# Scoring the two heads of a sliding-window pair on two 64-row tiles of TensorE, with a projection slot between two halves of the scores

## The reference

```python
s = jnp.einsum('bnqhgd,bnshd->bnhgqs', qb, kk) * scale      # 128 queries against 256 keys, per block and head
s = s - alibi_slopes(B_QHEADS).reshape(...) * dist
s = jnp.where(valid[None, :, None, None], s, NEG)
p = sink_softmax(s, sinks)                                  # softmax over the keys and one sink logit
o = jnp.einsum('bnhgqs,bnshd->bnqhgd', p, vv)
```

## Time and profile before

| what | value |
|---|---|
| three runs | 1378.04, 1379.92, 1379.98 us (median 1379.92) |
| span of the profiled execution, first to last instruction | 1374.8 us |
| the median run less this span | 5.1 us |
| TensorE busy, mean granted clock | 1324.7 us (96%), 0.991 |
| VectorE, ScalarE, GpSimd busy | 602.9, 519.1, 259.8 us |
| the sliding stage, 8 pairs | 775.6 us to about 1082 us |

### The profile page before, as it was taken

How to read it: one execution, slowest core, us unless ns; L and a number is a source line. 1 busy time by engine, 2 the same in 40 slices (tenths; PEclk the granted TensorE clock), 3 DMA queues, 4 the chain that set the end, 5 groups by cost and what they waited for, 6 DMA issues and landing times.

```text
span 1374.8 us, 23499 instructions
## 1 busy us (share of the span) xinstructions
PE 1324.7 (96%) x9150; PEld 1252.4 (91%) x9150; DVE 602.9 (44%) x1239; ACT 519.1 (38%) x1022; POOL 259.8 (19%) x119
## 2 busy tenths in 40 slices
PE   5799999999999999999999999999999999999998
PEld 4799999999999999899999988988988899999885
DVE  6636566574746465500000444555554400445222
ACT  6343635445353535511111434455444422313111
POOL 0222222222322222222222111011011022242000
PEclk9899999999999999999999999999999999999999
DMA  5212121202021221111112310111110312141231
GB/s 190 64 31 64 32 64 32 76 17 76 17 76 47 62 63 34 49 44 46 46 46 51 81 31 15 31 31 24 22 31 1 87 33 61 46 113 41 92 129 47
DMA packets 136750, 73.61 MB, mean 54 GB/s; under 512 B 37185, under 2 KB 133138, under 8 KB 136690
## 3 DMA queue, kind: packets, MB, share of 16 engines
q1 hardware_dynamic: 136706, 72.99, 19.0%
HBM read 63.77 MB, written 10.22 MB: 54 GB/s over the span
## 4 chain that ended last, share of the span: by engine, by line
PE 67%; issue 22%; POOL 5%; ACT 3%; DVE 3%; DMA 0%; SPq 0%; DVEq 0%; POOLq 0%; ACTq 0%
PE pj L970 46%; POOL w_l L556 4%; PE pj L986 3%; PE pj L1311 2%; PE ps_d L1201 1%; PE ps_e L1201 1%; PE ps_a L1311 1%; PE ps_e L1311 1%; PE ps_b L1189 1%; PE ps_c L1311 1%; PE ps_d L1311 1%; PE ps_b L1311 1%; PE ps_a L1189 1%; PE ps_a L1166 1%; PE ps_c L1189 1%
## 5 line engine op out<-in xcount | busy, mean ns | idle before, releaser
L970 PE MATMUL pj<-xn_h,w_h 128*128 128x352 f32 x1704 | 562.6, 330 | 10.9 <-DVE q L1384 5.3
L970 PE MATMUL pj<-xn_h,w_l 128*128 128x352 f32 x1704 | 552.0, 324 | 0.0
L970 PE MATMUL pj<-xn_l,w_h 128*128 128x352 f32 x1704 | 551.7, 324 | 0.0
L556 POOL TENSOR_TENSOR w_l<-w_raw,w_h 128x1024 fp32r<-128x1024 f32 x82 | 202.2, 2466 | 731.0 <-ACT w_h L628 731.0
L970 PEld LDWEIGHTS pj<-xn_h,w_h 128*128 128x128 f32 x1704 | 324.3, 190 | 15.7 <-DVE q L1384 5.6
L970 PEld LDWEIGHTS pj<-xn_l,w_h 128*128 128x128 f32 x1704 | 324.8, 191 | 0.3
L970 PEld LDWEIGHTS pj<-xn_h,w_l 128*128 128x128 f32 x1704 | 323.7, 190 | 0.0
L628 ACT ACTIVATE w_h<-w_raw 128x1024 fp32r<-128x1024 f32 x82 | 86.4, 1054 | 114.7 <-PE pj L970 99.8
L1546 DVE TENSOR_TENSOR mg<-sg,pj 128x352 f32 (+1 forms) x24 | 12.4, 522 | 151.7 <-PE pj L970 150.2
L837 ACT ACTIVATE scores<-scores,stat 128x256 f32<-128x256 f32 (+1 forms) x128 | 61.4, 481 | 0.0
L970 PE MATMUL pj<-hl_h,w_l 128*128 128x352 f32 x168 | 54.3, 323 | 0.0
(11 more groups left out here) (363 smaller groups left out, 2095.6 us busy)
## 6 DMA issues: line engine op xcount, KB each, us to landing
w_raw<-in_w_in_dram SPq DMA_DIRECT2D x132, 256.0 KB, 3.4
x_t<-in_x_prompt_dram SPq DMA_DIRECT2D x8, 512.0 KB, 8.5
s<-in_state_hgrn_dram SPq DMA_DIRECT2D x8, 512.0 KB, 4.2
out_dram<-s SPq DMA_DIRECT2D x8, 512.0 KB, 3.2
w_raw<-in_w_pa_dram SPq DMA_DIRECT2D x16, 256.0 KB, 2.9
w_raw<-in_w_pb_dram SPq DMA_DIRECT2D x16, 256.0 KB, 4.4
wo_raw<-in_w_out_dram SPq DMA_DIRECT2D x8, 512.0 KB, 4.0
x_o<-in_x_prompt_dram SPq DMA_DIRECT2D x8, 512.0 KB, 4.1
```

The lines of the kernel that those rows point to most:

```text
L556: g.tensor_tensor(w_l[p][:], w_raw[p][:], w_h[p][:].bitcast(F32), ALU.subtract).then_inc(w_lo_ready, 1)
L970: mm = nc.tensor.matmul(pj[g][:, 0:W], w[:, kt, :], x[:, kt, span(g)], start=(kt == 0 and m == 0), stop=(kt == KT - 1 and m == 2))
```

## The change

- The keys are kept once: `kT` is `[128, 1056]`. A score matmul takes 64 rows of `qT` and of `kT`: rows 0 to 63 for head 0, 64 to 127 for head 1, and the two heads of a block write different banks. The zero fill of `kT` in the prologue goes, three of six copies of the keys on ScalarE, and two of four transposes for the cache output.
- The scores go by quarters of two blocks (`scores_of(k)`): quarters 0 and 1, a slot, quarters 2 and 3, a slot.
- `sk` goes (VectorE and ScalarE read `sinks` directly); `qs` and `zs` go to ScalarE, ahead of the exponentials.
- Outs and turns go in rounds of three blocks, with one slot of the next gate between rounds.
- The loops over pairs are written out on TensorE, VectorE and ScalarE.

```diff
-        score_bank = lambda n, h: ((ps_a, ps_b, ps_c, ps_d)[n % 4], h * 2 * P)
+        head_rows = lambda h: slice(h * HD, (h + 1) * HD)
+        score_bank = lambda n, h: ((ps_a, ps_b, ps_c, ps_d)[n // 2 % 2 * 2 + h], n % 2 * 2 * P)
...
-                for n in range(NC):
-                    if n >= 4:
-                        t.wait_ge(dve_done, dve.at(now, f"t{2 * (n - 4) + 1}"))
-                    for h in range(2):
-                        bank, o = score_bank(n, h)
+                def scores_of(k):
+
+                    if k >= 2:
+                        t.wait_ge(dve_done, dve.at(now, f"t{QU * (k - 2) + QU - 1}"))
+                    for n in (2 * k, 2 * k + 1):
                         lo = P if n == 0 else 0
-                        mm = nc.tensor.matmul(bank[:, o + lo:o + 2 * P], qT[:, n * P:(n + 1) * P],
-                                              kT[:, h, (n - 1) * P + lo:(n + 1) * P], start=True, stop=True)
-                    mm.then_inc(pe_done, pe.tick(now, f"s{n}"))
+                        for h in range(2):
+                            bank, o = score_bank(n, h)
+                            mm = nc.tensor.matmul(bank[:, o + lo:o + 2 * P], qT[head_rows(h), n * P:(n + 1) * P],
+                                                  kT[head_rows(h), (n - 1) * P + lo:(n + 1) * P], start=True, stop=True)
+                    mm.then_inc(pe_done, pe.tick(now, f"s{k}"))
...
-                for g in range(2):
-                    next_slot(g)
+                scores_of(0)
+                scores_of(1)
+                next_slot(0)
+                scores_of(2)
+                scores_of(3)
+                next_slot(1)
...
-                for n in range(3):
+                for n in blocks_of(0):
                     turn(n)
                 next_slot(2)
-                for n in range(NC):
-                    out(n)
-                    if n + 3 < NC:
-                        turn(n + 3)
-                if not last:
-                    for g in range(SLOTS):
-                        t.wait_ge(act_done, act.at(now, f"q{g}"))
-                        slot(B(3), g)
+                for r in rounds:
+                    for n in blocks_of(r):
+                        out(n)
+                    for n in blocks_of(r + 1):
+                        turn(n)
+                    if not last:
+                        t.wait_ge(act_done, act.at(now, f"q{r}"))
+                        slot(B(3), r)
...
-                v.tensor_copy(sink_m[:].rearrange("p (h m) -> p h m", h=2), sinks[:].rearrange("p (h m) -> p h m", h=2)[:, :, bass.ds(m, 1)])\
-                 .then_inc(dve_done, dve.tick(now, "sk"))
-                v.wait_ge(dve_done, dve.at(now, "b1"))
-                v.tensor_copy(q_s[:, :, bass.ds(m, 1), :], qT[:, SEQ:T].rearrange("p (b o t) -> p b o t", b=NB, o=1)).then_inc(dve_done, dve.tick(now, "qs"))
```

More of the change, by code:

```diff
@@ L108, in hybrid_step @@
     exps = [x for k in quarters for x in [f"es0_{k}", f"es1_{k}"] + units("p", k)]
-    softmax = (["b0", "b1", "sk", "qs"] + [x for k in quarters for x in units("t", k) + [f"nm0_{k}", f"nm1_{k}"]] + ["zs"]
+    softmax = (["b0", "b1"] + [x for k in quarters for x in units("t", k) + [f"nm0_{k}", f"nm1_{k}"]]
                + [x for k in quarters for x in [f"dn{k}", f"rd{k}"] + units("n", k)])
-    turn_order = ["t0", "t1", "t2"] + [x for n in range(NC) for x in [f"o{n}"] + ([f"t{n + 3}"] if n + 3 < NC else [])]
+    blocks_of = lambda r: range(3 * r, min(3 * r + 3, NC))
+    rounds = range(3)
+    turn_order = [f"t{n}" for n in blocks_of(0)] + [x for r in rounds for x in [f"o{n}" for n in blocks_of(r)]
+                                                    + [f"t{n}" for n in blocks_of(r + 1)]]
     norms = ["rl0", "rl1", "rls", "rx"]
@@ L121, in hybrid_step @@
          + ["sigq1", "sigq2"] + each_slot("sigz"), HEADS - 1, len(norms)),
-        ("last", norms + exponentials + turned + [f"k{g}{h}" for g in range(SLOTS) for h in "ab"] + squares_of_head
+        ("last", norms + exponentials + turned + each_slot("k") + squares_of_head
          + each_tile("h", 0, 3) + each_slot("sg") + each_tile("h", 3, 5) + ["fl0", "fl1", "fls", "fx"] + each_tile("h", 5), 1, 0),
@@ L163, in hybrid_step @@
         ("kv", ["vt0", "vt1", "vts", "kt"], 1, 0),
-        ("swa", [f"s{n}" for n in range(NC)] + turn_order, HEADS - 1, 0),
-        ("swa_l", [f"s{n}" for n in range(NC)] + turn_order, 1, 0),
+        ("swa", [f"s{k}" for k in quarters] + turn_order, HEADS - 1, 0),
+        ("swa_l", [f"s{k}" for k in quarters] + turn_order, 1, 0),
         ("swa_s", ["ct0", "ct1", "s0", "s1", "s2", "s3", "pt", "pn", "o"], 1, 0),
@@ L743, in head @@
                         a.wait_ge(slot_done, B(1)[0] * 3 + (g + 1))
-                        for h in range(2):
-                            rows_h = slice(h * HD, (h + 1) * HD)
-                            a.activation(kT[rows_h, h, span(g)], pj[g][rows_h, 0:W], ACT.Copy).then_inc(act_done, act.tick(now, f"k{g}{'ab'[h]}"))
+                        a.activation(kT[:, span(g)], pj[g][:, 0:W], ACT.Copy).then_inc(act_done, act.tick(now, f"k{g}"))
                     split_hi(B(3))
@@ L816, in _ @@
             a.wait_ge(pe_done, pe.at(here, "kt"))
-            two_heads = lambda a: a.rearrange("p (h x) -> p h x", h=2)[:, :, 0:HD]
-            a.activation(k_out[:, 0, :].rearrange("p (h d) -> p h d", h=2), two_heads(ps_d[:, 0:6 * HD]), ACT.Copy).then_inc(act_done, act.tick(here, "kt"))
-            a.activation(k_out[0:NS, 1, :].rearrange("p (h d) -> p h d", h=2), two_heads(ps_e[0:NS, 0:6 * HD]), ACT.Copy).then_inc(act_done, act.tick(here, "ks"))
+            a.activation(k_out[:, 0, :], ps_d[:, 0:P], ACT.Copy).then_inc(act_done, act.tick(here, "kt"))
+            a.activation(k_out[0:NS, 1, :], ps_e[0:NS, 0:P], ACT.Copy).then_inc(act_done, act.tick(here, "ks"))
             split_hi(qz(2))
@@ L844, in pair @@
                 if not last:
-                    a.wait_ge(pe_done, pe.at(now, "s7"))
-                    a.wait_ge(dve_done, dve.at(now, "qs"))
+                    a.wait_ge(pe_done, pe.at(now, "s3"))
+                    a.wait_ge(act_done, act.at(now, "qs"))
                 for g in range(2):
@@ L849, in pair @@
                 for n in range(0, NC, 2):
[L850 removed]
+                    if n == 4:
                         queries(2)
@@ L865, in pair @@
                     split_hi(B(5))
-            with nc.scalar.Fori(0, HEADS - 1) as m:
+            for m in range(HEADS):
                 pair(m)
-            pair(HEADS - 1)
             here = ("swa_s", 0)
@@ L1037, in gate_slot @@
                         return
-                    step = f"k{g}b" if last and k_block == 2 else f"{name}{g}"
+                    step = f"k{g}" if last and k_block == 2 else f"{name}{g}"
                     t.wait_ge(by[0], by[1].at(now, step))
@@ L1143, in _ @@
             nc.tensor.transpose(ps_c[0:NS, 0:P], zb[:, SEQ:T], ident[:, :]).then_inc(pe_done, pe.tick(here, "vts"))
[L1144 to L1147, removed]
+            nc.tensor.transpose(ps_d[:, 0:P], kT[:, SEQ - P:SEQ], ident[:, :])
+            nc.tensor.transpose(ps_e[0:NS, 0:P], kT[:, SEQ:T], ident[:, :]).then_inc(pe_done, pe.tick(here, "kt"))
             for g in range(SLOTS):
@@ L1203, in out @@
                     mm.then_inc(pe_done, pe.tick(now, f"o{n}"))
-                for n in range(3):
+                for n in blocks_of(0):
                     turn(n)
                 next_slot(2)
-                for n in range(NC):
-                    out(n)
-                    if n + 3 < NC:
-                        turn(n + 3)
-                if not last:
-                    for g in range(SLOTS):
-                        t.wait_ge(act_done, act.at(now, f"q{g}"))
-                        slot(B(3), g)
+                for r in rounds:
[6 more added lines that the diff above has]
+                        slot(B(3), r)
             t.wait_ge(act_done, act.at(("kv", 0), "ks"))
             t.wait_ge(dve_done, dve.at(("kv", 0), "vt1"))
-            with nc.tensor.Fori(0, HEADS - 1) as m:
+            for m in range(HEADS):
                 pair(m)
-            pair(HEADS - 1)
             here, gb = ("swa_s", 0), Blocks(GB, 2, 0)
@@ L1243, in _ @@
                     nc.tensor.matmul(bank[32 * j:32 * j + 32, o:o + P], q_m, ckT[rows_h, m, :], start=True, stop=True)
-                    mm = nc.tensor.matmul(bank[32 * j:32 * j + 32, o + P:o + P + NS], q_m, kT[rows_h, h, SEQ:T], start=True, stop=True)
+                    mm = nc.tensor.matmul(bank[32 * j:32 * j + 32, o + P:o + P + NS], q_m, kT[rows_h, SEQ:T], start=True, stop=True)
                 mm.then_inc(pe_done, pe.tick(here, f"s{u}"))
@@ L1562, in _, with negate @@
                 gated(here, "z", g, zb)
-            def negate(now, k, new, old, sink, scores_next=len(quarters)):
+            def negate(now, k, new, old, sink):
```

(10 more changed lines are left out.)

34 lines of the change are left out of this document (16 added, 18 removed).

## The result

The changed kernel takes **1344.55 us** (median of 4 runs, 1343.57 to 1347.82), the kernel before beside it 1379.95 (1378.04 to 1381.16): a ratio of 0.9747, 95% interval 0.9732 to 0.9762. That is 35.4 us faster; 33.5 were forecast, and the time lies in the range.

A forecast was written before the change was run, and what follows sets the result against it. TensorE, busy 96% of the span, bounds the kernel. A pair saves 1.65 + 2.9 + 0.2 - 0.5 = 4.25 us; eight save 34.0, less 0.5 in the last, 33.5: 1346.4 us, range 1339 to 1361.

The forecast's parts named there:

- the new wait: TensorE ahead of turn 2 waits for VectorE's division of block 2: about 0.5 us a pair, between 0 and 1.2.
- the scores: Two 64-row tiles side by side take a pair's score matmuls from 6.5 to 3.6 us: 2.9 us saved.
- the loops: Pair loops written out: neither fetching new code nor the jump back shows, so nothing was counted.
- the stop: In each pair block 4's score matmuls wait for VectorE to empty a bank: 1.65 us saved, refill included.
- The ratio of the outs: Outs on two column halves take 0.57 of the whole-array time a record; used to estimate the row tiles' overlap.
- Boundaries: Changes between array shapes on TensorE, 0.12 us each, go from 12 to 10 a pair: 0.2 us saved.
- The last pair: No slot stands between rounds there, so two outs wait for copies of their turns: about 0.5 us lost once.
- Rival 1: The two row tiles of the score matmuls do not overlap: 1365.6 us; no or half an overlap has chance 0.17.
- Rival 3: VectorE's chain is late, the wait ahead of turn 2 takes 3 to 4 us: about 1378, no change; chance 0.03.
- Rival 2: The granted clock falls to the 1.2 GHz level in two slots a pair: 27 us slower, 1407; chance 0.05.

The follow-up runs named there:

- whole rows: Changed kernel with its scores on all 128 rows against doubled, zero-padded keys, order, halves and copies kept: 1358.63 us, ratio 0.9853.
- early division: Changed kernel with quarter 0 divided on VectorE ahead of reading quarters 2 and 3: 1340.60 us (ratio 0.9713), timed again 1340.28 (0.9726).
- One row tile: Changed kernel with head 1 also scored on rows 0 to 63, with head 0's queries and keys: 1365.08 us, ratio 0.9891.
- scores in one piece: Changed kernel with all four quarters of the scores ahead of slots 0 and 1, no slot between the halves: 1372.78 us, ratio 0.9945.

## Why the prediction was right

The account of a pair, by differences of one kernel to the next: loops written out 0.30, copies off VectorE 1.25, the order of slots and rounds 1.20, the tiles (whole rows against early division, both without a wait at the turns) 2.45, together 5.20; less 0.61 for the new wait, 4.59 us. These are differences along one chain of kernels, so they add up to the 4.59 from 39.76 to 35.17 by construction; what they show is the share of each step. By the means of seven pairs the whole is 4.56 and the loops' share 0.25.

The forecast had 4.25 a pair. It lies 0.34 too low: the gain of the scores was put 0.35 too low and that of the loops 0.30, while the stop and the new wait together were put some 0.25 too well. So the forecast of the time is closer than its terms, and part of that is luck.

- **The stop**, 1.65: right. Copies 1.25, and 0.27 of refill that goes only with the slot between, make 1.5; the loops add 0.06. As forecast the units run at their usual 0.29 us beside GpSimd, the `nm` behind them is held (1.08 us, until 853.91, 4.0 into the pair), and TensorE doesn't see it.
- **The scores**, 6.5 to 3.6: the overlap was right, the term too small. Steps of 0.215 make 3.25 us, so the overlap is worth 3.25, not 2.9. One row tile against early division, both without a wait at the turns and with the same boundaries, measures it by itself: 37.74 less 34.56 is 3.18. The ratio of the outs was the wrong neighbour. The Trainium skill (TensorEngine Tiling (Array Packing), Theoretical Speedup) gives up to 2x, and the trace reaches it.
- **Boundaries**, 0.2 saved: the sum right by luck, its parts not. The outs and turns save 0.9 by having six fewer, not 0.7; four new ones around row tiles cost 0.73, not 0.48. The Trainium skill (the same page, Key Properties) has a drain at each change of tiling mode; slots of 4.02 behind row tiles and 3.87 behind whole rows agree.
- **The new wait**, 0.5: right in place and cause; 0.28 as a wait, 0.61 as what its removal gives. (A third of 5.37 is 1.79, not the 1.76 of the working; 1.76 comes out without the copy `zs` that stands ahead of 905.83, and the wait moves by less than 0.1.)
- **The loops**, nothing: wrong by 0.25 to 0.30 us a pair, 2 to 3 us in all. The step compared the first pass with a repeated one, and both ran inside the loop, so the comparison could not show what a loop costs each time. What in the loop costs TensorE 0.2 us was not separated.
- **The last pair**, 0.5 lost: the stage gained 35.9, eight pairs at 4.59 make 36.7, so 0.8 (0.6 by the means); the one wait listed is 0.2. Not followed further.

Rival 1 (no overlap) is refuted by the records 0.01 us apart; the kernel on one tile came to 1365.1, and the rival's price was 1365.6. Rival 3's wait is 0.3, not 3. Rival 2's clock stays at 1.00 in the pairs of the change. A fall of the clock inside the pairs does occur here, but only in the kernel with its scores in one piece, where TensorE stalls between the tiles.

## What to carry to other kernels

Two 64-row tiles side by side halved the time of matmuls with 64 rows here, but each stretch of them paid about 0.18 us on either side, so keep the stretches long and few. Where an engine waits for a reader, put independent work between the halves rather than only making the reader faster: here it hid the wait and kept TensorE from stopping. Then look into the idle time that the reader has there; here it took in about half of a division of 1.34 us, and gave the next 5 us.

## What the runs showed of the hardware that was not expected

- A record of one row tile ran ahead of three earlier ones of the other tile; the order of the two heads within a quarter cost 0.12 us a pair.
- Matmuls of 64 rows on one tile take as long as those of 128 (0.43 us for two records of 256 columns), and pay the boundaries besides: 0.73 us a pair slower.
- Two stops of TensorE, 1.2 and 1.4 us, among small matmuls went with a granted clock at the 1.2 GHz level in some pairs, at up to 2.9 us a pair (40.10 for 37.24); in other pairs with the same two stops it stayed at 1.00. One stop of 1.4 us in the kernel before did not the earlier trace rows.
- A loop of seven passes on three engines cost 0.25 to 0.30 us a pass against the same code written out; what in the loop costs it was not separated.
